# Writing the sink values of the windowed attention group from ScalarE instead of VectorE

## The reference, cut to what matters

```python
m = jnp.maximum(jnp.max(logits, axis=-1, keepdims=True), sk)      # sk: the head's sink
p = jnp.exp(logits - m)
denom = jnp.sum(p, axis=-1, keepdims=True) + jnp.exp(sk - m)
p = (p / denom)
```

## Time and profile before

| | us |
|---|---|
| median of 3 runs (2323.56 to 2326.05) | 2325.01 |
| profiled execution | 2322.36 |
| its span | 2320.6 |
| PE busy | 2217.7 (96%) |
| DVE busy | 1441.1 (62%) |
| ACT busy | 921.0 (40%) |
| POOL busy | 332.9 (14%) |

### The profile page before, as it was taken

One profiled execution on the slowest core, in us unless ns is written; L12 is line 12 of the kernel. 1 busy time (PEld: TensorE's weight loads), 2 busy tenths in 40 slices (PEclk: granted clock), 3 DMA queues, 4 the chain that ended last, 5 costly groups with the idle time before them and its releaser, 6 DMA issues.

```text
span 2320.6 us, 33605 instructions
## 1 busy us (share of the span) xinstructions
PE 2217.7 (96%) x11592; PEld 1830.5 (79%) x11592; DVE 1441.1 (62%) x2761; ACT 921.0 (40%) x1790; POOL 332.9 (14%) x308
## 2 busy tenths in 40 slices
PE   6999999689999989969999999999999999999998
PEld 5888888677877768858888888788888878788886
DVE  5411023289899857768666565856565667666676
ACT  4311122178877733335333333533333333232333
POOL 6301300243334200002021202000000001010100
PEclk9999999899999999989999999999999999999999
DMA  8534333599953145665454546532323276353544
GB/s 243 163 136 132 96 100 96 149 246 242 237 137 108 55 167 195 229 230 210 159 200 161 201 155 243 182 133 78 127 80 125 76 286 239 110 177 109 177 150 153
DMA packets 278072, 376.78 MB, mean 162 GB/s; under 512 B 15578, under 2 KB 184546, under 8 KB 273328
## 3 DMA queue, kind: packets, MB, share of 16 engines
q1 hardware_dynamic: 269920, 354.21, 48.1%
q0 software_dynamic: 5568, 11.87, 2.1%
q10 hardware_dynamic: 2448, 8.91, 1.3%
HBM read 237.84 MB, written 140.31 MB: 163 GB/s over the span
## 4 chain that ended last, share of the span: by engine, by line
PE 51%; DVE 3%; DMA 1%; issue 0%; ACT 0%; DVEq 0%; ACTq 0%
PE ff_psum L1848 12%; PE ff_psum L1850 12%; PE ff_psum L1849 12%; PE ff_psum L1882 5%; PE ff_psum L1884 5%; PE ff_psum L1883 5%; DVE ff_a L1677 1%; DVE ff_x L1775 1%; DMA ff_raw<-in_w_gate 0%; DVE ff_d L1671 0%; DMA ff_d<-down_scratch 0%; DVE ff_ring L1658 0%; DVE ff_h L1663 0%; DVE ff_x L1788 0%; ACT ff_d L1547 0%
## 5 line engine op out<-in xcount | busy, mean ns | idle before, releaser
L1848 PE MATMUL ff_psum<-ff_h,ff_ring 128*128 128x512 f32 x1232 | 480.8, 390 | 14.8 <-DVE ff_ring L1658 12.5
L1849 PE MATMUL ff_psum<-ff_h,ff_ring 128*128 128x512 f32 x1232 | 480.4, 390 | 0.0
L1850 PE MATMUL ff_psum<-ff_h,ff_ring 128*128 128x512 f32 x1232 | 480.3, 390 | 0.0
L1848 PEld LDWEIGHTS ff_psum<-ff_h,ff_ring 128*128 128x128 f32 x1232 | 231.9, 188 | 63.5 <-DVEq L1724 12.9
L1849 PEld LDWEIGHTS ff_psum<-ff_h,ff_ring 128*128 128x128 f32 x1232 | 232.1, 188 | 48.6
L1850 PEld LDWEIGHTS ff_psum<-ff_h,ff_ring 128*128 128x128 f32 x1232 | 232.0, 188 | 48.1
L1882 PE MATMUL ff_psum<-ff_d,ff_a 128*128 128x512 f32 x616 | 240.6, 391 | 8.0 <-DVE ff_x L1775 5.3
L1883 PE MATMUL ff_psum<-ff_d,ff_a 128*128 128x512 f32 x616 | 239.7, 389 | 0.0
L1884 PE MATMUL ff_psum<-ff_d,ff_a 128*128 128x512 f32 x616 | 239.7, 389 | 0.0
L1775 DVE TENSOR_TENSOR ff_x<-ff_psum,ff_x 128x512 f32<-128x512 f32 x224 | 153.8, 689 | 123.5 <-PE ff_psum L1884 123.1
L1658 DVE TENSOR_TENSOR ff_ring<-ff_raw,ff_ring 128x512 fp32r<-128x512 f32 x176 | 130.0, 741 | 107.0 <-ACT ff_ring L1538 107.0
(11 more groups left out here) (149 smaller groups left out, 4100.2 us busy)
## 6 DMA issues: line engine op xcount, KB each, us to landing
acts_scratch<-ff_acts SPq DMA_DIRECT2D x22, 1792.0 KB, 7.9
ff_a<-acts_scratch SPq DMA_DIRECT2D x24, 960.0 KB, 5.0
ff_raw<-in_w_gate SPq DMA_DIRECT2D x42, 512.0 KB, 3.8
ff_raw<-in_w_up SPq DMA_DIRECT2D x42, 512.0 KB, 4.0
att_q_stack<-qk_scratch SPq DMA_DIRECT2D x64, 256.0 KB, 5.1
ff_d<-down_scratch SPq DMA_DIRECT2D x21, 768.0 KB, 6.3
ffn_in_scratch<-mix_h_stage SPq DMA_DIRECT2D x8, 1792.0 KB, 6.2
ff_h<-ffn_in_scratch SPq DMA_DIRECT2D x14, 1024.0 KB, 8.5
```

Source lines behind the costliest of these rows:

```text
L1848: pe.matmul(out_bank, whi[:, k], hhi[:, :, k], start=(k == 0 and not onto), stop=False, skip_group_check=onto)
L1849: pe.matmul(out_bank, whi[:, k], hlo[:, :, k], start=False, stop=False, skip_group_check=onto)
L1850: last = pe.matmul(out_bank, wlo[:, k], hhi[:, :, k], start=False, stop=(k == 3), skip_group_check=onto)
```

## The change

The eight small copies of a windowed round move from DVE to ACT. A new stage `set_sinks` on ACT has lag 1 and works in the last eight units of the round before: after `exp` of unit u (24 to 31) it writes the next round's sinks into that unit's buffer. DVE's shift still waits for `sink_set` in its first eight units. The negation of the sinks, and with it the wait for `win_in`, moves from unit 0 of round 4 to the start of DVE's stream, ahead of round 0. `may_set` is a counter that nothing waits for, as `may_shift` was.

```diff
@@ block.scalar
+            def set_sinks(kind, r, u):
+                if u < UNITS - SN_BUFS or (isinstance(r, int) and (r < NEAR_ROUNDS - 1 or r == ROUNDS - 1)):
+                    return
+                if kind.near and not isinstance(r, int):
+                    return
+                i = u % SN_BUFS
+                if isinstance(r, int) and kind.near and u == UNITS - SN_BUFS:
+                    act.wait_ge(sinks_negated, 1)
+                act.wait_ge(exped, SN_BUFS + UNITS * r + u + 1)
+                act.sem_inc(may_set, 1)
+                nc.scalar.copy(sn[:, i, 0:W:W - 1],
+                               sinks[:, bass.ds(r + 1 - NEAR_ROUNDS + 4 * (u % 2), 1)].broadcast_to([P, 2])) \
+                    .then_inc(sink_set, 1)
...
-            stream(act, [(TURN_LAG, copy_turned), (0, exp)])
+            stream(act, [(TURN_LAG, copy_turned), (1, set_sinks), (0, exp)])
@@ block.vector, in shift
-                    if isinstance(r, int) and r == NEAR_ROUNDS and u == 0:
-                        dve.wait_ge(win_in, 32)
-                        nc.vector.tensor_scalar(sinks[:], sinks[:], -1.0, None, ALU.mult).then_inc(sinks_negated, 1)
-                        dve.wait_ge(sinks_negated, 1)
                     if u < SN_BUFS:
-                        dve.sem_inc(may_shift, 1)
-                        nc.vector.tensor_copy(sn[:, i, 0:W:W - 1],
-                                              sinks[:, bass.ds(r - NEAR_ROUNDS + 4 * e, 1)].broadcast_to([P, 2])) \
-                            .then_inc(sink_set, 1)
                         dve.wait_ge(sink_set, SN_BUFS * (r - NEAR_ROUNDS) + u + 1)
@@ block.vector, ahead of the stream
+            dve.wait_ge(win_in, 32)
+            nc.vector.tensor_scalar(sinks[:], sinks[:], -1.0, None, ALU.mult).then_inc(sinks_negated, 1)
             stream(dve, [(NORM_LAG, invert), (0, shift), (NORM_LAG, normalise), (OUT_LAG, results)])
```

More of the change, by code:

```diff
@@ L19 @@
+from collections import namedtuple
 from contextlib import ExitStack
@@ L596, in attention_phase @@
         scored, shifted, exped = sem("scored"), sem("shifted"), sem("exped")
-        sink_set, may_shift = sem("sink_set"), sem("may_shift")
+        sink_set, may_shift, may_set = sem("sink_set"), sem("may_shift"), sem("may_set")
         summed, probs_done = sem("summed"), sem("probs_done")
```

## The result

The changed kernel takes 2330.65 us, median of 18 runs (2327.47 to 2332.24); the kernel before took 2325.81 in 18 runs beside it. The ratio is 1.0019, 95% interval 1.0013 to 1.0026: slower by 3 to 6 us. The prediction was 2337, 12.1 us slower; it had the sign and the place, and the loss it gave was more than twice too large.

What follows compares the result with a forecast made beforehand. The prediction took DVE to bound the windowed rounds. It summed + 28.4 (delay) - 6.3 (given back) - 12 (DVE's copies) + 2 (ACT) = + 12.1 us on the median of 2325.01, forecasting 2337 us, range 2328 to 2346.

Steps and rivals of the forecast that it cites:

- Part 3: Start of attention: DVE's first shift waits for the sinks' transfer, landing at 492.0, and comes 28.4 us late.
- Part 4: Round 0: stalls ahead of 492, PE's for keys and a long normalise, go and give back 6.3 us.
- Parts 1 and 2: Windowed rounds: 32 copies leaving DVE save 12 us; the same copies on ACT cost 2 us.
- the copies' places: DVE, windowed rounds: each copy puts its shift back 0.37 us, 11.8 us for 32.
- the long waits: DVE's copies: some 6.9 us of long ones, taken as waits for POOL that move to the normalise, saving nothing.
- ScalarE's charge: ACT, last eight units of rounds 4 to 6: the new copies just about fill idle time; 2 us charged.
- B: DVE, windowed rounds: long waits for POOL go with the copies; + 5.2 us, 2330; chance 0.10.
- C: Head of DVE's stream: sinks arrive early, not slower; landed by 480.4 us, the time is 2325; chance 0.04.
- A: ACT takes DVE's place at the rounds' ends and round 0 gives back little; + 21.5 us, 2346.5; chance 0.14.
- D: Windowed rounds' heads: sinks set late, DVE waits, spending 0.37 us a unit again; + 21.5 us, 2346.5; chance 0.03.
- the signs named for a wrong prediction: First shift before 485, round 0 at 48 us, windowed gain under 5 or over 15, rounds 1-3 off over 1 each.

Runs made afterwards that it cites:

- e1: Changed kernel with the win_in wait and negation moved from the head of DVE's stream to unit 8 of round 3; 2311.76 us, ratio 0.9941.
- e2: Kernel before with only the win_in wait and negation moved to the head of DVE's stream, sink copies still on DVE; 2341.97 us, ratio 1.0075.
- e3: Changed kernel with the transfers of window mask and sinks issued first in SP's list, ahead of round 0's loads; 2310.86 us, ratio 0.9938.
- e6: Kernel before with POOL's preparation of the output weights held back until the last shift of round 7, so POOL is silent in the windowed rounds; 2362.26 us.
- e10: e6 with the second of the two score matmuls left out in the windowed rounds, sink copies on DVE; 2357.21 us.
- e9: e7 with the second of the two score matmuls left out in the windowed rounds; 2348.71 us.
- e7: e1 with POOL's preparation of the output weights held back until the last shift of round 7; 2358.90 us.
- e5: e1 with ACT writing sinks only for round 4, the other 24 copies and DVE's waits for them left out; 2310.97 us, ratio 0.9939.
- e4: e1 with ACT writing each sink pair twice, with a wait for the first copy in between; 2317.30 us, ratio 0.9962.

## Why the prediction was wrong

- **The place and the sign** were right. The wait for two transfers at the end of SP's list decides (e1, e2, e3), and round 0 gives a part back.
- **Part 3, the delay**, was 26.4 us instead of 28.4. The landing was taken from the kernel before, 11.4 us after issue, and came after 9.7; the negation held the shift up by 0.27 instead of 0.5, and the phase began slightly sooner.
- **Part 4, given back**: 7.1 instead of 6.3. Both stalls went, and the first eight shifts took 6.96 us against 12.09 in the earlier trace rows.
- **Parts 1 and 2, the windowed rounds**, were 10 us net and came to 13.5, in the copies' places, the long waits and ScalarE's charge together. This is the largest miss, 3.5 of the 6.3 us by which the sum at the end of attention was off. The step that failed is the first conclusion on it: "So a windowed round is DVE's, and an instruction taken off DVE there is time". With POOL silent that holds for the first eight units of a round while the copies stand there (10.33 us in e6 and e10 alike); the rest of the round, and all of it once the copies are gone, goes at PE's pace (144.8 us falls to 129.6 in e9). The copies' own places are worth 5.2 us of the 11.8 booked (e6, e7). The waits for POOL were booked at nothing, because they would only move; they are worth 7.4. They did move in part, 3.0 of 6.9 us, but DVE without the copies makes up for most of them under PE's work; that last link is argued from the pairs, not isolated. ScalarE's 2 us were nothing (e5: 0.2). That two errors of opposite sign, 6.6 us too much for the places and 7.4 too little for the waits, left a fair total for DVE, 13.5 where 12 was booked, is luck.

The Trainium skill's rule in "SBUF — State Buffer", "Who interferes with whom", holds here: with POOL silent no copy and no normalise is long, and with POOL at work 3.0 us of the copies' 6.9 pass to the normalises. What I drew from it, that a wait which moves costs the same, is not in the rule, and the runs refute it.

Of the rivals, B has the total nearly right, + 5.2 us, with a mechanism that the runs don't bear out. C would have needed a landing before 480.4, and e3_loads_first is that case by another way: there the sinks are on the chip at 452.6, and the time falls to 2310.86. A and D didn't come: the last eight units of round 5 take 8.82 us with ScalarE's copies or without, and the first eight units of rounds 4 to 7 take 8.7 to 9.9. The stated range, 2328 to 2346, held the measured time near its low edge, and none of the signs named for a wrong prediction came; they were too wide to catch errors that cancel.

Reading again shows what was missed: PE's 37.81 us busy of 41.13 in round 4 stood beside DVE's 38.61, and DVE was taken for the bound; its 0.93 us between shifts was read as the round's pace, where 41.13 / 32 is 1.29 a unit. DVE's busy time held its waits for POOL, which the rows show as work. Without them DVE had far less, 132.56 of 150.00 in e6_before_quiet, and PE 146.89.

## What to carry to other kernels

When a one-time preparation is hoisted to the head of an in-order stream, everything behind it inherits the arrival of its inputs: look where their transfers stand in the issuing queue, and move them ahead or leave the preparation late. Here either way turned + 4.8 us into - 14 or - 15. An engine's busy time can hold waits for a shared port, so take the bound of a stage from a run or a stretch without them. A stall that moves to another instruction need not keep its price: here it fell with the room that the engine had to catch up.

## What the runs showed of the hardware

- An issue on SP behind many loads holds SP itself: 6.77 and 3.38 us for transfers of 192 and 4 KB behind the loads of round 0 (the changed kernel), 0.34 and 0.42 ahead of them (e3). The 4 KB landed 9.5 to 11.4 us after issue in the one case and 2.6 in the other.
- A copy of two columns on ScalarE takes 0.198 us, and eight in a stretch of eight units cost nothing. A second copy of each, with its wait, costs 5.5 us over the 32 (e4).
- POOL at work costs the windowed rounds 12.1 us with the sink copies on DVE (before, e6) and 4.7 without them (e1, e7). The waits on DVE, which the profile counts as its busy time, are by estimate 20.8 us in the kernel before and 16.9 in the changed one.
